# Six ring slots for gathers where there were eight, and two weight pairs kept for the second half of the prompt

## The chip, the cores and the metric

The kernel runs on one core of one Trainium2 chip. The metric is the device time of one execution in microseconds; the time of a kernel is the median of its runs.

## What is computed

One inference step of a small decoder with two layers, for a prompt of 512 tokens and eight samples of one token, all in float32 with a model width of 1024. Layer 0 mixes tokens with a gated short convolution and a dilated attention of eight heads, layer 1 with causal pooling. What takes most of the time stands in both layers after that: a retrieval of single-neuron experts. Each token makes eight queries, scores them against two sets of 128 subkeys, takes the 16 best of the 128 x 128 experts per head, and adds up 16 x 8 rows of a table, each weighed by the gelu of its dot product with the token:

```python
def peer_ffn(h, wq, subkeys, u_tab, v_tab):
    ...
    q = (hb @ wq).reshape(chunk, PEER_HEADS, 2, PEER_HALF)
    s = einsum('nhcd,hckd->nhck', q, sk)
    sv, si = top_k(s, 16)
    cs, ci = top_k(sv[:, :, 0, :, None] + sv[:, :, 1, None, :], 16)
    expert = i1 * 128 + i2
    act = gelu(einsum('nd,nhkd->nhk', hb, u_tab[expert]))
    return einsum('nhk,nhkd->nd', softmax(cs) * act, v_tab[expert])
```

## The kernel before, in words

The prompt's 512 tokens are four tiles of 128, one token to a partition; the first half of the prompt is tiles 0 and 1, the second half tiles 2 and 3. A *task* is one head of one tile, 16 *uses*; the samples' task at the end of each layer has eight. That makes 520 uses to a layer and 1040 in all. For each use GpSimd (POOL) gathers one expert for every token: 128 rows of 2048 floats, the expert's row of `u` and of `v` side by side, into one slot of `RING` (line 937). Slot `use % SLOTS` is used over and over, and the gather waits until the use `SLOTS` before it has been worked off (lines 932 to 935: `v_freed` from TensorE, `x_freed` for the few that VectorE adds itself). When the rows have landed, VectorE makes the dot products (line 2041), ScalarE the gelu, the gate and a diagonal matrix of the gates (lines 1502, 1507, 1511), and TensorE multiplies the diagonal with the rows of `v` into an accumulator (line 1310), which frees the slot.

All other work (the projections, attention and pooling of a half prompt, the queries and their scores) is cut into *pieces*. `agenda()` puts the pieces between the uses: while the experts of one half are being summed, the pieces of the next half are worked off. Every engine goes through the same list of pieces in order, SyncE (SP) too.

SP loads the weights. They come in pairs of 128 columns each, 1 MB a pair. `pair_homes()` gives each pair a buffer (its *home*): homes 0 and 1 are the two buffers of `WCH`, 2 and 3 lie in the ring's memory before the gathers begin, and 4 to 7 are places in `SC`, `H`, `VN` and `KT` that are free once, for four of layer 0's query pairs. For `WCH` a pair is loaded as soon as TensorE has closed the last piece that used the pair before it in that home (`AFTER`, in SP's `front`). A layer has eight query pairs (16 chunks, pieces `("q", l, b, hc)`); each half of the prompt (`b` = 0, 1) needs all eight. Before, every half loads all of them.

Until `ring_cleared` (set by VectorE once the samples' rows of the first mixer have been stored) the ring's memory holds other things. POOL's first gather waits for it, and for the first indices. POOL then issues in order, and SP, too, issues in order: a wait there holds all loads and small moves that stand behind it. Among those are the moves of the samples' scores from `YT` to `SC` (line 835).

Of the kernel before, what the change touches and what calls it, by code (L numbers as in the profile page):

```python
# [30 lines left out]
P = 128  # L31
D = 1024
KD = D // P
# [10 lines left out]
HC = 2 * PH  # L44
# [12 lines left out]
NW_FIRST = 4  # L57
NW_ONCE = 4
# [3 lines left out]
HT_N = BN + B  # L62
NB = 5
ACC_BANKS = (6, 4)
SLOTS = 8
ROW = 2 * D
DVE_LAG = 3
ADD_AT = 3
# [176 lines left out]
EARLY = 4  # L245
# [144 lines left out]
def pair_homes():  # L390

    chunks = chunk_list()
    cut = chunks.index(("q", 0, 0, 0)) // 2
    last, homes, after = {}, [], {}
    for n in range(len(chunks) // 2):
        once = n - cut - NW
        if 0 <= once < NW_ONCE:
            homes.append((NW_FIRST + once, 0))
            continue
        usable = range(NW_FIRST if n < cut else NW)  # L400
        home = min(usable, key=lambda b: last.get(b, b - NW_FIRST))
        if home in last:
            after[last[home]] = n
        last[home] = n
        homes.append((home, sum(h == home for h, _ in homes)))
    return homes, after
# [14 lines left out]
def build(nc, x_prompt, x_sample, state_conv, state_win_k, state_win_v, state_pool, norm_mix, w_in_ab,  # L421
# [5 lines left out]
    with ctx:  # L427
        def sb(name, shape, dt=f32):
            return ctx.enter_context(nc.sbuf_tensor(name, shape, dt))

        def sem(name):
            return ctx.enter_context(nc.semaphore(name))
# [3 lines left out]
        Hv = H[:, :].rearrange("p (s d) -> p s d", d=D)  # L436
        HT = sb("HT", [P, KD, HT_N])
        SC = sb("SC", [P, T * HC * NK + 2 * NK])
        RING = sb("RING", [P, SLOTS * ROW])
        WCH = sb("WCH", [P, NW, 2, KD, WC])  # L440
        KT = sb("KT", [P, CA, SEQ])
        VN = sb("VN", [P, T, DA])
# [54 lines left out]

        rows = RING[:, :].rearrange("p (s n) -> p s n", n=ROW)
        hrep = (H[:, BT * D + D:BT * D + 2 * D], KT[:, :, :].rearrange("p c n -> p (c n)")[:, 0:D])

        KV = 2 * DA
        kv = RING[:, 0:NKV * KV].rearrange("p (a t n) -> p a t n", a=NKV, t=2)
        o = NKV * KV
# [44 lines left out]
        o += B  # L548
        own_probs = RING[0:B * NH, o:o + NH]
        o += NH  # L550
        assert o <= SLOTS * ROW

        UW = BN + 2
        o = BT * HC * NK
# [35 lines left out]
        CHUNKS = chunk_list()  # L590
        HOMES, AFTER = pair_homes()
# [8 lines left out]
        g_loaded = sem("g_loaded")  # L600
        small_loaded = sem("small_loaded")
        sk_loaded = sem("sk_loaded")
        w_loaded = [sem(f"w_loaded{n}") for n in range(NW_FIRST + NW_ONCE)]
        kv_loaded = [sem(f"kv_loaded{n}") for n in range(NKV + 2)]
        pool_loaded = sem("pool_loaded")
        sample_moved = [sem(f"sample_moved{n}") for n in range(2)]
# [32 lines left out]
        sexp_ready = sem("sexp_ready")  # L639
        landed = [sem(f"landed{s}") for s in range(SLOTS)]  # L640
        ring_cleared = sem("ring_cleared")
# [46 lines left out]
        def pair_buffer(home):  # L688

            once = home - NW_FIRST  # L690
            if home < NW:
                return WCH[:, home, :, :, :]
            if home < NW_FIRST:
                return wch_first[:, home - NW, :, :, :]
            area = H[:, 3 * D:5 * D] if once == 2 else SC[:, (2 + once) * 2 * D:(3 + once) * 2 * D]
            return area.rearrange("p (t k n) -> p t k n", t=2, k=KD)

# [18 lines left out]
        def wait_chunk(eng, piece):  # L716
            n, which = divmod(CHUNKS.index(piece), 2)
            home, use = HOMES[n]
            eng.wait_ge(w_loaded[home], 16 * (use + 1) if home < NW_FIRST + 3 else 32)
            return [chunk_column(home, which, k) for k in range(KD)]  # L720

        block = ctx.enter_context(nc.Block())
# [2 lines left out]
        def _(sp):  # L725
# [5 lines left out]
            def load_pair(n):  # L731
                piece = CHUNKS[2 * n]
                if piece[0] == "p":
                    src = w_in_ab[0, ("bcxqkv".index(piece[2]) * CA + piece[3]) // 2]
                elif piece[0] == "v":
                    src = w_in_ab[0, (5 * CA + piece[2]) // 2]
                elif piece[0] == "wo":
                    src = w_out_ab[0, piece[2] // 2]
                else:
                    src = peer_wq[piece[1], piece[3] // 2]  # L740
                home = HOMES[n][0]
                if home == NW_FIRST + 3:
                    for which in range(2):
                        part = split_chunk(which)
                        sp.dma_start(part, src[:, which, :, :].rearrange("p (a b) n -> p a b n", a=part.shape[1])
                                     ).then_inc(w_loaded[home], 16)
                else:
                    sp.dma_start(pair_buffer(home), src).then_inc(w_loaded[home], 16)
# [26 lines left out]
            def front(piece):  # L775
                kind = piece[0]
                if piece == ONCE_AT:
                    wait_full(sp, piece)
                    for n in range(len(HOMES)):
                        if HOMES[n][0] >= NW_FIRST:  # L780
                            load_pair(n)
                if piece in CHUNKS and CHUNKS.index(piece) % 2 and CHUNKS.index(piece) // 2 in AFTER:
                    wait_full(sp, piece)
# [13 lines left out]
                if kind == "kn":  # L797
                    t = piece[1] * BT + piece[2]
# [17 lines left out]
                if kind == "so" and piece[1] in (4, 5):  # L816
                    t = BT + piece[1] - 4
# [59 lines left out]
        def _(pool):  # L877
# [51 lines left out]
            def gather(tau, k):  # L929

                use = first(tau) + k
                if use >= SLOTS and by_vector(use - SLOTS):
                    pool.wait_ge(x_freed, vector_rows(use - SLOTS) + 1)
                elif use >= SLOTS:
                    pool.wait_ge(v_freed, tensor_rows(use - SLOTS) + 1)
# [1259 lines left out]
```

## Time and profile before

| | us |
|---|---|
| median of 3 runs | 2979.59 |
| lowest and highest run | 2979.23, 2981.12 |
| the profiled execution | 2981.27 |
| its span (first to last instruction) | 2979.3 |
| PE busy | 2586.0 (87%) |
| VectorE busy | 2077.1 (70%) |
| GpSimd busy | 1223.5 (41%) |
| moved by DMA | 1213.29 MB, mean 407 GB/s |

The first gather is issued at 214.6 us, layer 0's uses end near 1640 us, and the rest is layer 1. Busy shares are means over the whole run; the part from 214 us on, in which the gathers run, is read by itself below. A PE that is busy 87% has its own waits inside that, since the ends of matmuls are modelled. "To landing" of a DMA is the time from its issue to its last byte's semaphore.

### The profile page before, as it was taken

What the parts mean: (1) busy time and instruction counts of PE and PEld (TensorE: products, weight loads), DVE (VectorE), ACT (ScalarE), POOL (GpSimd) and SP (SyncE); (2) the same over time, 40 slices, a digit from 0 to 9 for tenths busy, and PEclk for the clock granted to TensorE, in tenths of its full rate; (3) what the DMA queues carried; (4) which work ended last, traced back from release to release, by engine and by line L of the source; (5) the groups of instructions that cost most, each with busy time, mean ns of one, the idle gap of its engine ahead of it and who ended that gap; (6) DMA issues with size and microseconds to landing.
All of it is one profiled execution on the core that took longest, in us unless ns stands there. A gap on an engine that the chain in (4) does not pass through costs nothing.

```text
span 2979.3 us, 26395 instructions
## 1 busy us (share of the span) xinstructions
PE 2586.0 (87%) x7285; PEld 1274.0 (43%) x7285; DVE 2077.1 (70%) x4938; ACT 1281.6 (43%) x3753; POOL 1223.5 (41%) x1104
## 2 busy tenths in 40 slices
PE   8999998999988888888988888788999978778787
PEld 7675564555444443334444333333444422222222
DVE  3657766887766667776667677777666766677666
ACT  2123435655434435444444444445443444444444
POOL 2013543444444434444444444445434444444442
PEclk9999999999999999999999999999999999999999
DMA  9979999999999999999999999999999999999997
GB/s 356 366 278 381 405 421 412 422 400 406 421 421 421 421 420 396 421 421 421 421 421 421 411 410 414 421 418 414 416 421 420 419 416 412 421 419 417 421 414 331
DMA packets 174565, 1213.29 MB, mean 407 GB/s; under 512 B 19685, under 2 KB 20721, under 8 KB 32843
## 3 DMA queue, kind: packets, MB, share of 16 engines
q0 software_dynamic: 155904, 1124.11, 91.6%
q1 hardware_dynamic: 18515, 87.51, 7.6%
q8 instruction: 58, 0.95, 0.1%
q14 instruction: 88, 0.72, 0.1%
HBM read 1206.90 MB, written 38.37 MB: 418 GB/s over the span
## 4 chain that ended last, share of the span: by engine, by line
DMA 46%; PE 36%; DVE 8%; ACT 6%; issue 3%; POOL 1%; ACTq 0%; POOLq 0%; DVEq 0%
DMA RING<-in_peer_uv,idx 45%; PE PSUM L1310 22%; PE PSUM L989 9%; DVE RING L2041 4%; ACT diag L1511 2%; ACT L1502 1%; ACT gate L1507 1%; DMA RING<-in_peer_uv,pidx 1%; PE PSUM L1000 1%; POOL RING L937 1%; PE PSUM L971 1%; ACT act_h L1502 1%; ACT L1490 1%; PE PSUM L1298 1%; PE PSUM L1088 0%
## 5 line engine op out<-in xcount | busy, mean ns | idle before, releaser
L1310 PE MATMUL PSUM<-RING,diag 128*128 128x512 f32 (+1 forms) x4032 | 1955.0, 622 | 359.7 <-ACT diag L1511 353.7
L937 POOL DMA_INDIRECT RING<-in_peer_uv,idx x1024 | 1171.8, 1144 | 1544.3 <-PE PSUM L1310 1413.2
L2041 DVE CUSTOM_DVE_ANT_0 RING<-RING,H 128x1024 f32<-128x1024 f32 x1032 | 1262.7, 1224 | 700.8 <-DMA RING<-in_peer_uv,idx 694.7
L1310 PEld LDWEIGHTS PSUM<-RING,diag 128*128 128x128 f32 (+1 forms) x4032 | 732.9, 193 | 1420.9 <-ACT diag L1511 784.3
L1502 ACT ACTIVATE act_h<-dots 128x1 f32<-128x1 f32 x1040 | 208.1, 200 | 1110.4 <-DVE dots L2041 1108.9
L1511 ACT ACTIVATE diag<-ident,gate 128x128 f32<-128x128 f32 x992 | 398.3, 402 | 33.0 <-PE PSUM L1310 0.5
L989 PE MATMUL PSUM<-HT,WCH 128*128 128x256 f32 (+2 forms) x1408 | 335.0, 385 | 1.4 <-ACT HT L1363 1.3
L989 PEld LDWEIGHTS PSUM<-HT,WCH 128*128 128x128 f32 x1408 | 266.5, 193 | 94.5 <-issue 62.7
L1507 ACT ACTIVATE gate<-act_h,ex 128x1 f32<-128x1 f32 x992 | 292.2, 295 | 32.3
L1502 ACT ACT_TABLE_LOAD x90 | 115.5, 1283 | 5.6 <-DVE dots L2041 4.0
L1363 ACT ACTIVATE YT<-PSUM 128x256 f32<-128x256 f32 (+4 forms) x70 | 27.3, 391 | 173.2 <-PE PSUM L989 157.8
L2041 DVE DVE_READ_ACCUMULATOR2_ANT dots<- 128x1 f32 x1040 | 85.9, 83 | 0.0
L1490 ACT ACT_TABLE_LOAD x66 | 84.7, 1283 | 1.2
L1382 ACT ACTIVATE H<-H,negm 128x128 f32<-128x128 f32 (+3 forms) x32 | 18.0, 562 | 97.8 <-DVE negm L1743 97.6
L1298 PEld LDWEIGHTS PSUM<-SKT,YT 128*128 128x128 f32 (+1 forms) x316 | 41.4, 172 | 33.8 <-issue 29.6
L1298 PE MATMUL PSUM<-SKT,YT 128*128 128x128 f32 (+1 forms) x316 | 49.2, 279 | 0.0
L971 PE MATMUL PSUM<-ident,H 128*128 128x128 f32 (+1 forms) x200 | 33.6, 288 | 17.2 <-POOL POOL_STATE_M L886 9.7
L926 POOL DMA_DIRECT2D out_win_v_sample<-in_state_win_v x16 | 9.8, 617 | 91.5 <-PE PSUM L989 58.5
L989 PE MATMUL PSUM<-HT,RING 128*128 128x264 f32 x192 | 44.6, 389 | 0.0
L2019 DVE TENSOR_TENSOR onehot<-cij,iota 128x512 f32<-128x512 uint32 x65 | 44.6, 687 | 0.0
L2022 DVE TENSOR_TENSOR onehot<-onehot,si 128x512 f32<-128x512 f32 x65 | 44.6, 686 | 0.0
L2024 DVE TENSOR_REDUCE picked<-onehot 128x32 f32<-128x512 f32 x65 | 44.3, 681 | 0.0
(265 smaller groups left out, 1533.7 us busy)
## 6 DMA issues: line engine op xcount, KB each, us to landing
WCH<-in_peer_wq SPq DMA_DIRECT2D x28, 1024.0 KB, 9.1
WCH<-in_w_in_ab SPq DMA_DIRECT2D x18, 1024.0 KB, 9.8
RING<-in_peer_uv,idx POOLq DMA_INDIRECT x1024, 15.0
out_win_k_sample<-in_state_win_k POOLq DMA_DIRECT2D x8, 2016.0 KB, 12.7
out_win_v_sample<-in_state_win_v POOLq DMA_DIRECT2D x8, 2016.0 KB, 11.9
RING<-in_w_in_ab SPq DMA_DIRECT2D x6, 1024.0 KB, 11.5
WCH<-in_w_out_ab SPq DMA_DIRECT2D x6, 1024.0 KB, 9.8
X<-in_x_prompt SPq DMA_DIRECT2D x4, 512.0 KB, 4.3
```

The lines of the kernel that those rows point to most:

```text
L937: pool.indirect_dma_start(rows[:, use % SLOTS, :], None, peer_uv.rearrange("l e n -> (l e) n"), bass.IndirectOffsetOnAxis(ap=at, axis=0),) ...
L971: last = nc.tensor.transpose(out[0:cols, n * width:n * width + rows], src, ident[0:rows, 0:rows])
L989: last = nc.tensor.matmul(out[:, lo:width], w[k], rows[:, k, lo:width], start=(k == 0), stop=(k == KD - 1))
L1298: last = nc.tensor.matmul(out[0:m, j * P:(j + 1) * P], qp[:, hc % 2, j * P:j * P + m], SKT[:, hc, :], start=True, stop=True)
L1310: last = nc.tensor.matmul(PSUM[0:out_n, accumulator(n) + half, :], diag[:, at % DIAGS, 0:out_n], rows[:, use % SLOTS, D + half * 512:D + h ...
L1490: nc.scalar.activation(ex[:, par, :], cs[:, par, :], ACT.Exp, bias=ncs[:, par:par + 1], accum_out=exsum[:, par:par + 1]).then_inc(gates_ex ...
L1502: chain(nc.scalar.activation(act_h[:, st, column], dots[:, st, column], ACT.Gelu))
L1507: chain(nc.scalar.activation(gate[:, st, column], act_h[:, st, column], ACT.Copy, scale=weight))
L1511: nc.scalar.activation(diag[:, at % DIAGS, 0:n], selector, ACT.Copy, scale=gate[:, st, column]).then_inc(diag_ready, 1)
L2019: left(V.tensor_tensor(onehot[:], cij[:].unsqueeze(3).to_broadcast([P, 2, TOP, TOP]), iota16[:].unsqueeze(1).unsqueeze(1).to_broadcast([P, ...
L2022: left(V.tensor_tensor(onehot[:], onehot[:], si[:].unsqueeze(2).to_broadcast([P, 2, TOP, TOP]), ALU.mult))
L2041: V.tensor_tensor_reduce(out=u, in0=u, in1=row, scale=1.0, scalar=0.0, op0=ALU.mult, op1=ALU.add, accum_out=dots[:, tau % SETS, k:k + 1]). ...
```

## The change

`SLOTS` goes from 8 to 6, so a gather waits for the use six before it. The two slots that come free stay in `RING` behind the six, as homes 8 and 9. They hold the query pairs of heads 6 and 7, which are chunks 12 to 15. Layer 0's are loaded once SP comes to the piece `("sc", 0, 0, 3)`, after a wait for `ring_cleared`, and layer 1's once layer 0's second half has used the old ones. Both halves of the prompt multiply with them; the second half loads none for these chunks. Since six of the eight query pairs now go through the other homes, the second half's input pairs move up in `WCH`.

```diff
-SLOTS = 8
+SLOTS = 6
+KEPT = 2
...
     for n in range(len(chunks) // 2):
+        kind, *at = chunks[2 * n]
+        kept = at[2] // 2 - (HC // 2 - KEPT) if kind == "q" else -1
+        if kept >= 0:
+            home = NW_FIRST + NW_ONCE + kept
+            if at[1] == 0 and home in last:
+                after[last[home]] = n
+            last[home] = n
+            homes.append((home, at[0]))
+            continue
...
-        RING = sb("RING", [P, SLOTS * ROW])
+        RING = sb("RING", [P, (SLOTS + KEPT) * ROW])
...
+            if once >= NW_ONCE:
+                kept = SLOTS + once - NW_ONCE
+                return RING[:, kept * ROW:(kept + 1) * ROW].rearrange("p (t k n) -> p t k n", t=2, k=KD)
...
-            eng.wait_ge(w_loaded[home], 16 * (use + 1) if home < NW_FIRST + 3 else 32)
+            eng.wait_ge(w_loaded[home], 32 if home == NW_FIRST + 3 else 16 * (use + 1))
...
-                        if HOMES[n][0] >= NW_FIRST:
+                        if NW_FIRST <= HOMES[n][0] < NW_FIRST + NW_ONCE:
                             load_pair(n)
+                if piece == ("sc", 0, 0, EARLY - 1):
+                    sp.wait_ge(ring_cleared, 1)
+                    for n in range(len(HOMES)):
+                        if HOMES[n][0] >= NW_FIRST + NW_ONCE and CHUNKS[2 * n][1:3] == (0, 0):
+                            load_pair(n)
```

On SP, where the gathers begin, before (`in_peer_wq` are query pairs, `in_w_in_ab` input pairs of the second half, a row of 128x2048 is one pair of 1 MB):

```order
L748 DMA WCH<-in_peer_wq 128x2048
L835 DMA SC<-YT 8x256 x2
L748 DMA WCH<-in_peer_wq 128x2048
L835 DMA SC<-YT 8x256 x10
L748 DMA WCH<-in_w_in_ab 128x2048
L835 DMA SC<-YT 8x256 x2
L748 DMA WCH<-in_w_in_ab 128x2048
L835 DMA SC<-YT 8x256 x2
```

and now:

```order
L761 DMA WCH<-in_w_in_ab 128x2048
L853 DMA SC<-YT 8x256 x2
L761 DMA WCH<-in_w_in_ab 128x2048
L761 DMA RING<-in_peer_wq 128x2048 x2
L853 DMA SC<-YT 8x256 x14
```

The two input pairs stand where the two query pairs stood, and the two query pairs follow them into the ring's memory ahead of the small moves.

On SP, at the second half of layer 1, before:

```order
L748 DMA WCH<-in_peer_wq 128x2048
L835 DMA SC<-YT 8x256 x2
L748 DMA WCH<-in_peer_wq 128x2048
L835 DMA SC<-YT 8x256 x2
L748 DMA WCH<-in_peer_wq 128x2048
L835 DMA SC<-YT 8x256 x2
L748 DMA WCH<-in_peer_wq 128x2048
L835 DMA SC<-YT 8x256 x2
L748 DMA WCH<-in_peer_wq 128x2048
L835 DMA SC<-YT 8x256 x2
L748 DMA WCH<-in_peer_wq 128x2048
L835 DMA SC<-YT 8x256 x6
```

and now:

```order
L761 DMA WCH<-in_peer_wq 128x2048
L853 DMA SC<-YT 8x256 x2
L761 DMA WCH<-in_peer_wq 128x2048
L853 DMA SC<-YT 8x256 x2
L761 DMA WCH<-in_peer_wq 128x2048
L853 DMA SC<-YT 8x256 x2
L761 DMA WCH<-in_peer_wq 128x2048
L853 DMA SC<-YT 8x256 x10
```

Of the loads between the moves of this half, the last two are gone; layer 0's second half loses two in the same way.

On POOL, the first gathers, before (the names in brackets are the semaphores that the instruction waits for):

```order
L937 DMA RING<-in_peer_uv,idx 128x2048 [waits first_picked,ring_cleared]
L937 DMA RING<-in_peer_uv,idx 128x2048 x7
L937 DMA RING<-in_peer_uv,idx 128x2048 [waits v_freed,idx_ready]
L937 DMA RING<-in_peer_uv,idx 128x2048 [waits v_freed] x5
L937 DMA RING<-in_peer_uv,idx 128x2048 [waits x_freed]
```

and now:

```order
L955 DMA RING<-in_peer_uv,idx 128x2048 [waits first_picked,ring_cleared]
L955 DMA RING<-in_peer_uv,idx 128x2048 x5
L955 DMA RING<-in_peer_uv,idx 128x2048 [waits v_freed] x2
L955 DMA RING<-in_peer_uv,idx 128x2048 [waits v_freed,idx_ready]
L955 DMA RING<-in_peer_uv,idx 128x2048 [waits v_freed] x3
L955 DMA RING<-in_peer_uv,idx 128x2048 [waits x_freed]
```

Six gathers go out at once where eight did, and from the seventh on each waits for a slot.

## Rows read from the trace of the kernel before

**Rows 1.** The page's slices: DMA share in tenths, and GB/s, 40 slices.

```profile
DMA  9979999999999999999999999999999999999997
GB/s 356 366 278 381 405 421 412 422 400 406 421 421 421 421 420 396 421 421 421 421 421 421 411 410 414 421 418 414 416 421 420 419 416 412 421 419 417 421 414 331
```

**Rows 2.** The page's chain that ended last, by engine and by line.

```profile
DMA 46%; PE 36%; DVE 8%; ACT 6%; issue 3%; POOL 1%; ACTq 0%; POOLq 0%; DVEq 0%
DMA RING<-in_peer_uv,idx 45%; PE PSUM L1310 22%; PE PSUM L989 9%; DVE RING L2041 4%; ACT diag L1511 2%; ACT L1502 1%; ACT gate L1507 1%; DMA RING<-in_peer_uv,pidx 1%; PE PSUM L1000 1%; POOL RING L937 1%; PE PSUM L971 1%; ACT act_h L1502 1%; ACT L1490 1%; PE PSUM L1298 1%; PE PSUM L1088 0%
```

**Rows 3.** Stretches: length, each engine's busy us (xcount), PE clock, DMA share, GB/s.

```profile
214.00:640.00 426.00, 394.14 (x1302) 229.51 (x1301) 314.46 (x760) 203.35 (x555) 180.09 (x151) 0.97 0.99 404
640.00:1300.00 660.00, 577.15 (x1631) 289.09 (x1630) 484.83 (x1114) 299.04 (x868) 287.54 (x247) 0.97 1.01 417
1300.00:1640.00 340.00, 304.24 (x828) 146.31 (x826) 231.85 (x565) 145.28 (x448) 145.74 (x130) 0.98 1.01 421
1640.00:2960.00 1320.00, 1109.04 (x2625) 462.11 (x2624) 931.83 (x2195) 584.11 (x1754) 577.55 (x513) 0.97 1.01 417
```

**Rows 4.** Line 937, its gathers in the same four stretches, in order.

```profile
L937 POOL DMA_INDIRECT RING<-in_peer_uv,idx x151: 932/940/2768, 214.6 to 637.8; - x151
DMA to landing us min/median/max: 5.4/11.9/19.9
DMA to landing us min/median/max: 5.8/14.5/23.7
DMA to landing us min/median/max: 10.1/15.7/18.8
DMA to landing us min/median/max: 9.6/15.3/20.6
```

**Rows 5.** Timeline of DVE, 1149 to 1162 us: start, us, what, idle before.

```profile
1151.07 1.23 DVE L2041 CUSTOM_DVE_ANT_0 RING<-RING,H 128x1024 f32<-128x1024 f32 x1 [0.48 <-DMA RING<-in_peer_uv,idx]
1153.53 1.23 DVE L2041 CUSTOM_DVE_ANT_0 RING<-RING,H 128x1024 f32<-128x1024 f32 x1 [0.35 <-DMA RING<-in_peer_uv,idx]
1156.01 1.23 DVE L2041 CUSTOM_DVE_ANT_0 RING<-RING,H 128x1024 f32<-128x1024 f32 x1 [0.38 <-DMA RING<-in_peer_uv,idx]
1159.08 1.22 DVE L2041 CUSTOM_DVE_ANT_0 RING<-RING,H 128x1024 f32<-128x1024 f32 x1 [1.43 <-DMA RING<-in_peer_uv,idx]
```

**Rows 6.** Timeline of POOL, two gathers, at 600 and at 1151 us.

```profile
600.77 0.94 POOL L937 DMA_INDIRECT RING<-in_peer_uv,idx  x1 [10.05 <-PE PSUM L1310]
...
1151.38 1.73 POOL L937 DMA_INDIRECT RING<-in_peer_uv,idx  x1 [0.30 <-PE PSUM L1310]
```

**Rows 7.** Line 937 in 236-316, 480-545, 595-722, 1135-1170, 1290-1300, 1800-1812 us.

```profile
DMA to landing us min/median/max: 6.4/8.7/10.0
DMA to landing us min/median/max: 8.9/10.7/15.9
DMA to landing us min/median/max: 5.4/9.9/12.2
DMA to landing us min/median/max: 5.8/8.5/14.8
DMA to landing us min/median/max: 9.0/9.8/10.1
DMA to landing us min/median/max: 9.6/10.0/10.9
```

**Rows 8.** Stretch 320 to 352 us, columns as in rows 3.

```profile
320.00:352.00 32.00, 32.00 (x104) 17.39 (x104) 20.92 (x50) 13.94 (x43) 15.41 (x13) 1.00 1.00 415
```

**Rows 9.** Timeline of SP's queue, 214 to 222 us.

```profile
218.41 1.41 SPq L835 DMA_DIRECT2D SC<-YT  x2
220.27 0.34 SPq L748 DMA_DIRECT2D WCH<-in_peer_wq  x1
```

**Rows 10.** Timeline of DVE, the copy of the samples' scores at 258 us.

```profile
258.27 0.27 DVE L1882 COPY YT<-PSUM 8x128 f32<-8x128 f32 x1
```

More of the change, by code:

```diff
@@ L550, in build @@
         o += NH
-        assert o <= SLOTS * ROW
+        assert o <= (SLOTS + KEPT) * ROW
         UW = BN + 2
@@ L602, in build @@
         sk_loaded = sem("sk_loaded")
-        w_loaded = [sem(f"w_loaded{n}") for n in range(NW_FIRST + NW_ONCE)]
+        w_loaded = [sem(f"w_loaded{n}") for n in range(NW_FIRST + NW_ONCE + KEPT)]
         kv_loaded = [sem(f"kv_loaded{n}") for n in range(NKV + 2)]
```

## The prediction

> **What bounds the kernel now.** I read the page's slices first, then the chain that ended last, then the stretches. From the fourth slice on the 16 DMA engines are busy nine tenths or more, and in many slices they move 421 GB/s [rows 1]. The chain that ended last is 45% waiting for the gathers into the ring and 36% PE [rows 2]. So the gathers' bytes set the pace: a gather is 128 rows of 8 KB, 1.049 MB, and 1.049 MB / 421 GB/s = 2.49 us. VectorE's products show it: where they wait for nothing but the landing they start 2.46 and 2.48 us apart [rows 5].
>
> The second thing to see is how far ahead the ring lets the gathers run. One lap of a slot has two parts: from issue to landing, and the rest (product, gelu, gate, diagonal, matmul, and POOL's next issue). The stretches give the pace [rows 3], the landings their median [rows 4]:
> - 214 to 640 us: 151 gathers in 426 us, 2.82 us each, a lap of eight 22.6 us; landing takes 11.9, the rest 10.7.
> - 640 to 1300: 2.67 each, lap 21.4, landing 14.5, rest 6.9.
> - 1300 to 1640: 130 in 340, 2.62 each, lap 20.9, landing 15.7, rest 5.2.
> - 1640 to 2960: 513 in 1320, 2.57 each, lap 20.6, landing 15.3, rest 5.3.
>
> The shortest landing of the run is 5.4 us [rows 4]: a gather issued into an empty queue. What a landing takes above 5.4 us is other transfers standing ahead, and that is the reserve that keeps the DMA engines busy while POOL waits for a slot.
>
> **The change part by part.**
>
> *Fewer bytes.* The order of SP shows four loads of 1 MB gone: each layer's last two query pairs are fetched for the first half of the prompt and not again for the second. One costs 2.49 us of the DMA engines. Layer 0's places in SP's order are taken by the loads behind them, which move up in `WCH`, so the queue is empty of two loads where the second half's first pairs of layer 1 stood, about 1640 us, and of the last two of layer 1. There the DMA share is full [rows 1, 3] and nothing else is the limit: 4 x 2.49 = 10.0 us gained, hidden only where the DMA engines stop for another reason.
>
> *Two loads move forward.* The second half's first two input pairs are now loaded at the places where before's query pairs 12 to 15 were, and these go into the ring behind `ring_cleared`. So 2 MB leave the stretch from 320 to 352 us, where the DMA share is full but PE too is busy 32.00 of 32.00 us [rows 8], and go to about 220 to 240 us. There six gathers are issued at first where it was eight, so the bytes up to there are the same ten MB. The gain is 0 if PE is the limit at 320 to 352, 2 x 2.49 = 5.0 us if DMA is; both are full there, I take the middle, 2.5.
>
> *The new wait on SP.* SP waits for `ring_cleared` ahead of these two loads. POOL's first gather, behind the same semaphore, is issued at 214.6 us [rows 4], and SP's instruction just ahead of the wait is the load at 220.27 us [rows 9], so the wait has ended before SP comes to it: nothing. Behind it on SP's queue stand the moves of the sample's scores, issued from 218 us on [rows 9]. Behind 2 MB that share the engines with gathers, they land up to 4 x 2.49 = 10 us later; the VectorE copy that needs the next pair of them out of the way is at 258.27 us [rows 10]. That is cover of over 20 us, so nothing again; without it the opening would lose up to 10 us. The tail of the change, where layer 1's kept pairs are loaded after layer 0's second half has used them, moves loads within the same stretch: nothing.
>
> *Two slots fewer.* This is the term to weigh. At the same pace a lap of six leaves for the landing: 16.9 - 10.7 = 6.2 us from 214 to 640, 16.0 - 6.9 = 9.1 to 1300, 15.7 - 5.2 = 10.5 to 1640, 15.4 - 5.3 = 10.1 after. Against 5.4 needed, layer 1 keeps nearly 5 us to spare and the first stretch 0.8. So the loss sits in layer 0's first half and wherever POOL was held up for long, as at 600.77 us, where it had waited 10.05 us for PE [rows 6].
>
> To size it, go by the dips. A gather that lands L after its issue had L - 5.4 us of queue ahead of it. Two slots fewer take 2 x 2.49 = 4.98 us out of the queue, so the engines stand still for 10.4 - L wherever L is under 10.4. Each dip is charged once, at its shortest landing [rows 7]: 236 to 316 us: 10.4 - 6.4 = 4.0; 480 to 545: 1.5; 595 to 722: 5.0; 1135 to 1170: 4.6; about 1295: 1.4; about 1807: 0.8. Sum 17.3 us. Once lost, the time is given to every gather behind it, so a dip is not charged per gather.
>
> Upward: two dips are long. The first holds 28 gathers, 4.7 laps of six, with a median of 8.7 us: 1.7 per lap is 8.0, 4.0 more than charged. The third holds 45 gathers and may empty the queue twice, 5.0 more. That makes 26.3. A row also says that 5.4 is too kind: the gather issued at 1151.38 [rows 6] came 4.6 us ahead of the product at 1156.01, and yet its own product starts 3.07 us after that one and not 2.48 [rows 5], so the pace is lost 0.6 us earlier than 5.4 gives it; 0.6 for six dips is 3.6, together 30. Downward: the first stretch has PE busy 394 of 426 us [rows 3], and if PE hides the first two dips, 17.3 - 5.5 = 11.8. All of it vanishes only if the rest of a lap shrinks as landings come later, which it can where a landed row lay waiting for VectorE. I take the middle of 17.3 and 26.3, 21.8, since the long dips are long in the rows, and the PE that would hide them is what makes POOL wait.
>
> The shortest landing in the rows is 5.4 us [rows 4]. The Trainium skill, "DMA: Bandwidth & Descriptors", section "Anatomy of one DMA — SWDGE (gpsimd) path", gives a transfer issued by GpSimd 2.0 us plus its bytes at 436 GB/s; for a gather that is an estimate of 4.4 us, and no gather of this trace landed under 5.4. By 4.4 the threshold would be 9.4 and the dips 3.0 + 0.5 + 4.0 + 3.6 + 0.4 = 11.5 us, which with the two gains would make the change even. The measured 5.4 decides.
>
> *Sum:* 21.8 - 10.0 - 2.5 = +9.3 us. On the profiled execution of 2981.27 us (span 2979.3 and 2.0 around it) that is 2990.6; the median of the runs is 1.7 lower, 2979.59, so 2988.9, called 2989.
>
> **The rivals.**
> 1. *The ring was deeper than needed* (ends faster). The point is the rest of the lap from 214 to 640 us: 10.7 us, of which much may be rows that had landed and waited for VectorE and PE. If later landings take it from that waiting, six slots turn over in time, and the loss stays under 6.5 us; at 2.5 the sum is -10.0, 2969.6. For it: PE is near full there [rows 3]. Against it: landings of 5.4 and 5.8 us, an empty queue already with eight slots [rows 4, 7]. 0.13.
> 2. *A draw.* Only the dips outside PE's full stretches count, 11.8, and 11.8 - 12.5 = -0.7: 2979, and within 0.2% (6 us, about what a measurement can tell from no change) for losses from 6.5 to 18.5. 0.25.
> 3. *Every lap of the first stretch is short.* If each of the 151 / 6 = 25 laps lacks the 1.7 us of the first dip, that is 43, with the three later dips 4.6 + 1.4 + 0.8 = 50, and +37 in the sum: 3017. Against it: half the gathers there land in over 11.9 us [rows 4], above the threshold. 0.08.
> 4. That the four loads don't go: excluded by the order of SP.
>
> **How the numbers follow.** My forecast, a loss of 18.5 to 30 against 12.5 or less gained, +6 to +20 us or 2986 to 3000 with 2989 the likeliest, has 0.54. Slower is this with rival 3, 0.62; same 0.25; faster 0.13. The range leaves out rival 1 and most of rival 3: 2974 to 3003.
>
> **What would show it.** Right: four weight loads fewer; landings of the gathers near 10 us in layer 1 where they were 15.3, with the DMA share as full as before and that part some 10 us shorter; layer 0 longer by 10 to 20 us, with the DMA share lower from 214 to 720 and about 1140, and landings of 5.4 there more often. The forecast is wrong if layer 0 up to 1300 us keeps its length (rival 1), or if VectorE's waits for landings grow in layer 1 too.

## The result, and the profile after

The changed kernel takes 3027.14 us (median of five runs, 3022.52 to 3030.89); the kernel before, on the same chip, 2980.20 (2979.23 to 2981.15). The ratio is 1.0146, with an interval of 1.0136 to 1.0157: 46.9 us slower. The sign was forecast, the size (+9) was not. The profiled execution took 3022.52 us with a span of 3020.8, 41 more than before.

The page's slices of the kernel after, DMA share in tenths and GB/s, to be laid beside [rows 1], and the line of its packets:

```profile
DMA  9979999999999999999999999999999999999998
GB/s 352 365 284 385 377 415 393 369 364 353 416 412 409 416 422 393 419 395 418 422 421 417 396 402 401 421 417 415 417 414 419 418 413 421 419 414 420 418 413 356
DMA packets 173989, 1209.10 MB, mean 400 GB/s; under 512 B 19621, under 2 KB 20657, under 8 KB 32779
```

The bytes are 4.19 MB fewer, as the change says. But slices 7 to 10 (about 450 to 755 us) move 393, 369, 364 and 353 GB/s where they moved 412, 422, 400 and 406. The DMA share in tenths still reads 9 in all four: this digit hides a loss of a tenth, and GB/s shows it.

The stretches of the kernel after, columns as in [rows 3]:

```profile
214.00:420.00 206.00, 193.98 (x657) 116.40 (x656) 147.29 (x359) 84.12 (x251) 84.57 (x72) 0.98 0.99 385
420.00:500.00 80.00, 69.89 (x209) 39.25 (x208) 52.41 (x122) 35.71 (x98) 28.60 (x26) 0.94 1.01 414
500.00:580.00 80.00, 68.34 (x219) 37.62 (x218) 54.26 (x126) 43.63 (x105) 31.39 (x26) 0.96 0.94 361
580.00:680.00 100.00, 88.00 (x279) 48.26 (x277) 76.16 (x182) 51.35 (x127) 38.09 (x33) 0.95 0.93 371
680.00:760.00 80.00, 67.93 (x228) 38.57 (x229) 62.03 (x150) 41.10 (x100) 33.05 (x26) 0.94 0.92 353
...
1680.00:3000.00 1320.00, 1110.01 (x2633) 462.77 (x2633) 932.43 (x2199) 585.38 (x1759) 577.45 (x516) 0.98 1.01 414
```

And those of the kernel before that stand against the third to fifth:

```profile
500.00:580.00 80.00, 77.28 (x257) 43.12 (x258) 63.66 (x157) 52.13 (x127) 35.89 (x31) 1.00 1.00 413
580.00:680.00 100.00, 89.86 (x298) 50.03 (x296) 85.70 (x203) 56.53 (x137) 42.70 (x35) 0.95 0.99 406
680.00:760.00 80.00, 77.23 (x262) 45.26 (x260) 60.14 (x142) 39.36 (x107) 34.61 (x31) 0.98 0.99 408
```

The loss is local. Over these 260 us the kernel before moves 408.8 GB/s on average, the kernel after 362.4; to move the same bytes after takes 260 x 408.8 / 362.4 = 293 us, 33 more. No engine is fuller for it: PE, VectorE and ScalarE all do less. How much later than in the kernel before VectorE makes the product of a use, its shift, says the same (one execution of each kernel; the times in brackets are those of before). Use 96 (499 us) is 4.2 us late, use 192 (767 us) 36.0, use 416 (1360 us) 45.5, use 544 41.5, use 784 41.2 and the last 41.5. So 32 of 41 us are lost in uses 96 to 191, most of them with pieces of the second half's attention between them (these stand at uses 86 to 168), another 9.5 from there to 1360 us, and behind that 4.0 are given back, where layer 1's loads are gone.

The waits in that stretch, after (500 to 755 us; engine, line, what it waited for, us in total, times, longest):

```profile
POOL RING L955 <- PE PSUM L1328: 138.6, 66, 10.1
DVE RING L2059 <- DMA RING<-in_peer_uv,idx: 52.6, 42, 6.0
ACT act_h L1520 <- DVE dots L2059: 51.1, 30, 4.4
...
ACT H L1400 <- DVE negm L1761: 37.1, 13, 5.6
PEld PSUM L1328 <- ACT diag L1529: 22.5, 14, 4.1
```

The same uses in the kernel before (497 to 722 us):

```profile
POOL RING L937 <- PE PSUM L1310: 114.8, 62, 10.1
...
ACT act_h L1502 <- DVE dots L2041: 35.6, 20, 7.3
ACT H L1382 <- DVE negm L1743: 26.9, 13, 3.1
...
DVE RING L2041 <- DMA RING<-in_peer_uv,idx: 13.9, 21, 1.6
PEld PSUM L1310 <- ACT diag L1511: 13.0, 14, 2.8
```

VectorE's wait for landings goes from 13.9 to 52.6 us. But ScalarE waits longer for VectorE too, PE's weight loads for ScalarE, and POOL for PE. Every link of the way from a landing back to the next gather has grown, which is what a closed lap looks like: no engine is always busy, each waits for the next. But idle times grow in any stretch in which the same work takes longer, so the rows alone do not show a lap; the experiments have to.

The chain of waits of the kernel after shows one such lap (start, us, what; pieces between left out):

```profile
551.39 11.42 DMA RING<-in_peer_uv,idx
...
562.84 0.04 DVE RING L2059
...
564.68 0.48 DVE H L1757
...
565.18 0.56 DVE negm L1760
...
565.96 0.61 ACT H L1400
...
566.59 1.28 ACT L1520
...
568.45 0.41 ACT diag L1529
...
568.90 3.37 PE PSUM L1328 x4
572.27 1.73 PE PSUM L1007 x8
574.00 3.43 PE PSUM L1328 x8
...
581.41 1.45 POOL RING L955
...
583.17 8.55 DMA RING<-in_peer_uv,idx
```

A gather lands at 562.8 and VectorE makes its product (line 2059). Only behind that, in VectorE's order, stand the mask and the maximum of one attention step (lines 1757 to 1761), since VectorE's products run three uses ahead of the pieces (`DVE_LAG`). ScalarE's exponential (line 1400) waits for the maximum, and behind the exponential stand the gates and diagonals of rows that landed long before; behind the diagonals stand PE's matmuls, which free the slots. So a late landing holds back slots that have nothing to do with it.

What that does to the next gathers, POOL's timeline of the kernel after (start, us, what, idle before):

```profile
563.76 1.11 POOL L955 DMA_INDIRECT RING<-in_peer_uv,idx  x1 [0.78 <-PE PSUM L1328]
573.06 0.94 POOL L955 DMA_INDIRECT RING<-in_peer_uv,idx  x1 [8.18 <-PE PSUM L1328]
575.99 0.97 POOL L955 DMA_INDIRECT RING<-in_peer_uv,idx  x1 [1.99 <-PE PSUM L1328]
577.71 0.94 POOL L955 DMA_INDIRECT RING<-in_peer_uv,idx  x1 [0.75 <-PE PSUM L1328]
581.41 1.45 POOL L955 DMA_INDIRECT RING<-in_peer_uv,idx  x1 [2.77 <-PE PSUM L1328]
583.17 1.03 POOL L955 DMA_INDIRECT RING<-in_peer_uv,idx  x1 [0.30 <-issue]
```

and the last two products of those, on VectorE:

```profile
585.43 1.23 DVE L2059 CUSTOM_DVE_ANT_0 RING<-RING,H 128x1024 f32<-128x1024 f32 x1 [1.38 <-DMA RING<-in_peer_uv,idx]
...
589.22 1.23 DVE L2059 CUSTOM_DVE_ANT_0 RING<-RING,H 128x1024 f32<-128x1024 f32 x1 [1.62 <-DMA RING<-in_peer_uv,idx]
```

Worked out from the landing records, the four gathers issued at 573.06, 575.99, 577.71 and 581.41 land at 578.55, 581.88, 585.41 and 589.19: after 5.5, 5.9, 7.7 and 7.8 us, and each 3.3 to 3.8 us behind its predecessor instead of 2.49. This is where the forecast's threshold breaks. A landing of 7.7 us has over 2 us of queue ahead of it by my 5.4, and yet the pace was lost four times running.

The waits of layer 1 show nothing of the sort: VectorE waits for landings as in the kernel before. First after (1680 to 3000 us), then before (1640 to 2960 us):

```profile
DVE RING L2059 <- DMA RING<-in_peer_uv,idx: 370.3, 457, 3.8
```

```profile
DVE RING L2041 <- DMA RING<-in_peer_uv,idx: 371.2, 456, 3.5
```

### The profile page after: what moved, and what is told of

It reads as the page before. It is cut to its first block, busy times and chain, and to the rows that moved or that the text cites. A ratio compares the mean times of both kernels' runs of the same rounds, so it can differ in the third digit from the quotient of the medians.

```text
span 3020.8 us, 26391 instructions
## 1 busy us (share of the span) xinstructions
PE 2598.1 (86%) x7285; PEld 1274.3 (42%) x7285; DVE 2079.9 (69%) x4938; ACT 1285.5 (43%) x3753; POOL 1214.5 (40%) x1104
## 4 chain that ended last, share of the span: by engine, by line
DMA 40%; PE 38%; ACT 9%; DVE 8%; issue 3%; POOL 1%; SPq 0%; DVEq 0%; ACTq 0%; POOLq 0%
DMA RING<-in_peer_uv,idx 39%; PE PSUM L1328 24%; PE PSUM L1007 9%; DVE RING L2059 5%; ACT diag L1529 2%; ACT L1520 2%; ACT gate L1525 2%; ACT L1508 1%; ACT act_h L1520 1%; PE PSUM L989 1%; POOL RING L955 1%; PE PSUM L1316 1%; DMA RING<-in_peer_uv,pidx 1%; PE PSUM L1018 1%; PE PSUM L1106 0%
## 5 line engine op out<-in xcount | busy, mean ns | idle before, releaser
L1007 PE MATMUL PSUM<-HT,WCH 128*128 128x256 f32 (+2 forms) x1152 | 270.7, 382 | 1.6 <-ACT HT L1381 1.4
L1007 PEld LDWEIGHTS PSUM<-HT,WCH 128*128 128x128 f32 x1152 | 216.8, 192 | 75.7 <-issue 49.7
L1007 PE MATMUL PSUM<-HT,RING 128*128 128x264 f32 (+1 forms) x448 | 108.0, 390 | 0.0
L1007 PEld LDWEIGHTS PSUM<-HT,RING 128*128 128x128 f32 x448 | 84.1, 192 | 24.1 <-issue 12.5
L989 PEld LDWEIGHTS PSUM<-ident,H 128*128 128x128 f32 (+1 forms) x200 | 24.7, 156 | 54.1 <-DVE den L1768 20.6
## 6 DMA issues: line engine op xcount, KB each, us to landing
out_win_v_sample<-in_state_win_v POOLq DMA_DIRECT2D x8, 2016.0 KB, 11.2
```

Source lines behind the costliest of these rows:

```text
L989: last = nc.tensor.transpose(out[0:cols, n * width:n * width + rows], src, ident[0:rows, 0:rows])
L1007: last = nc.tensor.matmul(out[:, lo:width], w[k], rows[:, k, lo:width], start=(k == 0), stop=(k == KD - 1))
```

## The experiments

In all of them the ratio is to the kernel before on the same chip. The theories: **depth** (two slots fewer make the whole loss, the loads a gain of some 10), against something else in the change; then, once depth was seen, what in uses 96 to 191 makes it cost so much, the **engines' own load** or the **closed lap** of waits just read.

**Depth alone.** In the kernel before, with its eight slots and all its loads, a gather waits also for the use six (e1) or seven (e2) before it, and in e3 the use six before it in uses 96 to 191 alone:

```diff
-                if use >= SLOTS and by_vector(use - SLOTS):
-                    pool.wait_ge(x_freed, vector_rows(use - SLOTS) + 1)
-                elif use >= SLOTS:
-                    pool.wait_ge(v_freed, tensor_rows(use - SLOTS) + 1)
+                lag = 6
+                freed = dict.fromkeys(by_vector(use - n) for n in (SLOTS, lag) if use >= n)
+                for vector in freed:
+                    at = max(use - n for n in (SLOTS, lag) if use >= n and by_vector(use - n) == vector)
+                    if vector:
+                        pool.wait_ge(x_freed, vector_rows(at) + 1)
+                    else:
+                        pool.wait_ge(v_freed, tensor_rows(at) + 1)
```

(e2: `lag = 7`; e3: `lag = 6 if 96 <= use < 192 else SLOTS`.)

> The kernel before with its eight slots and all its weight loads, but each gather also waits for the use six before it, so that at most six are under way. If the ring's depth alone makes the loss, this shows the measured +47 us without the 10 us of saved loads: 3035 to 3042 us, with most of it between uses 96 and 192. If the kept pairs and the moved loads make it (a weight load that now stands in the way at the start, or of the second half's input pairs), this stays within 10 us of before, 2980 to 2990. By the sum of dips on record it would be 2980 + 22 = 3002.

> As the run with six, but each gather waits for the use seven before it. By the dips of the prediction one slot fewer moves the threshold to 7.9 us: 1.5 + 2.5 + 2.1 = 6 us, 2986. If every lap of the stretch of attention pieces pays, the seventh slot is worth a fifth to a half of what two are: 2990 to 3005.

> The wait for the use six before only in uses 96 to 191, in which the changed kernel's products fell back by some 30 us; eight elsewhere. If the loss is made there, +25 to +32: 3005 to 3012. If it is a slower rate of the DMA engines with fewer gathers under way, it is spread over the run and these 9% of the uses cost about 5 us: 2985.

Measured, against 2983.89 for the kernel before: e1 3043.58 (1.0195, 1.0178 to 1.0212), e2 2996.70 (1.0043, 1.0026 to 1.0060), e3 3017.39 (1.0112, 1.0093 to 1.0131). Depth alone costs 59.7 us at six and 12.8 at seven, so the second slot costs more than three times what the first does. The dips on record gave 22 and 6. Most of the price at six is paid in uses 96 to 191: the shift of e1's products goes from 10.1 to 45.7 us there, and e3, which has six only there, loses 33.5. The rest of the change (the moved loads, the new wait on SP, the kept pairs' places) is not needed to explain the sign, nor the place where most is lost.

**The loads alone.** e4 has eight slots and does not load the last two query pairs of each layer for the second half; the identity stands in for them:

```diff
+        if kind == "q" and at[1] == 1 and at[2] >= HC - 4:
+            homes.append((-1, 0))
+            continue
...
+            if home < 0:
+                return [ident[:, :]] * KD
```

> The kernel before with eight slots, but the second half's last two query pairs of each layer are not loaded: the four chunks are multiplied with the identity matrix, so those heads choose other experts. Four loads of 1 MB fewer and nothing else. If the DMA engines are the limit where they stood, 4 x 2.49 = 10 us less: 2970. If they are hidden, 2980.

Measured 2974.51 (0.9965, 0.9951 to 0.9979), 9.4 us faster; the sum said 10.0. e1's loss less this gain is 50.3, the change itself lost 46.9: the two parts account for it to within 3.4 us, less than the intervals of e1 and e4 leave open.

**One slot, one pair.** e9 is the change with `SLOTS = 7` and `KEPT = 1`.

> The changed kernel with seven slots and one kept pair per layer: two loads fewer in place of four. The wait for the use seven before cost 12.8 us by itself, two loads give back 5.0, the one moved load 0 to 2.5: 2985 to 2989 where before is 2980; by the sum on record (a dip rule with 7.9 us for a threshold, 6 us lost) about even, 2979.

Measured 2986.95 against 2982.15 (1.0016, 1.0006 to 1.0025): 4.8 us slower. Half the exchange loses as well, if little: e2's 12.8 less two loads, 5.0, would be 7.8.

**The engines' load.** e5 leaves out half of the matmul's columns in uses 96 to 191 on PE (but for a task's first and last use), e7 half of the dot product's columns on VectorE. These two have eight slots and serve as yardsticks; e6 and e8 are the same with the wait of e3.

```diff
-                for half in range(2):
+                for half in range(1 if 96 <= use < 192 and 0 < k < steps(tau) - 1 else 2):
```

```diff
+                if 96 <= use < 192:
+                    u, row = u[:, 0:D // 2], row[:, 0:D // 2]
```

> The kernel before, eight slots, but in uses 96 to 191 TensorE leaves out the second half of the sum's columns (512 of 1024), except in a task's first and last use. This is the yardstick for the next run: TensorE has some 80 us less to do there. The stretch is 2.8 us per use against 2.49 for its bytes, so at most 25 us can go: 2960 to 2975.

> The same columns left out, and the wait for the use six before in uses 96 to 191. If slots are lost because TensorE holds them while it works on the second half's attention, the 33 us that this wait cost in full shrink to under 15 beside the yardstick. If fewer gathers under way slow the DMA engines themselves, whoever holds the slots, the cost stays near 33.

> The kernel before, eight slots, but in uses 96 to 191 VectorE's dot product takes 512 of 1024 columns, some 0.55 us less per use, 51 us in all. Yardstick for the next run: 2960 to 2980.

> The same shorter dot product, and the wait for the use six before in uses 96 to 191. If VectorE is what holds the slots there, the 33 us shrink to under 15 beside its yardstick; if TensorE is, they shrink only by what a lap is shorter, to 20 to 30; if it is the DMA engines' own rate, they stay near 33.

Measured: e5 2981.50 (0.9994, 0.9983 to 1.0006), e6 3004.80 (1.0072, 1.0050 to 1.0095), e7 2980.93 (0.9994, 0.9983 to 1.0005), e8 3003.41 (1.0066, 1.0043 to 1.0089). The yardsticks did not fall, so with eight slots neither engine sets the time there, and my expectations missed, for e5 by 6 us and for e7 by 1. Six slots cost 23.3 us beside e5 and 22.5 beside e7, where they cost 33.5 in full: each relief takes a third. That is neither the 15 or less of an engine that holds the slots nor the 33 of a rate that the DMA engines set by themselves; only e8's bound of 20 to 30, for slots held by TensorE, was met, and e6 does not bear it out. e15 and e16 have both reliefs at once.

> The kernel before, in which uses 96 to 191 leave out half of the dot product's columns on VectorE and half of the columns of the matmul on PE (e5 and e7 together). It is the yardstick of e16: 2970 to 2982 us by either theory.

> e15 with the wait for the use six before in uses 96 to 191 alone. Theory of the engines' load (the two engines together fill the laps): each relief alone took ten of the 33.5 us, so both take twenty or more, and at most 14 us remain beside e15. Theory of the closed lap: the waits between the engines stay, and 16 us or more remain.

Measured: e15 2978.98 (0.9985, 0.9975 to 0.9995), e16 3000.21 (1.0047, 1.0030 to 1.0064). Still 21.2 us, with e16's four runs from 2996.02 to 3006.74. The work of both engines on the uses halved is worth no more than that of one, so this load is not what fills the lap, and that theory fell by its own bound of 14. One limit: PE was relieved by less than the columns left out, 32 us of busy time in e15, since its granted clock fell too. From 500 to 755 us the kernel before, e15 and e16 read:

```profile
500.00:755.00 255.00, 239.37 (x797) 135.53 (x798) 205.40 (x490) 146.63 (x364) 110.63 (x93) 0.97 1.00 408
```

```profile
500.00:755.00 255.00, 207.46 (x680) 123.52 (x679) 161.89 (x497) 148.11 (x367) 96.65 (x96) 0.89 1.00 414
```

```profile
500.00:755.00 255.00, 198.30 (x628) 115.39 (x626) 151.25 (x458) 140.91 (x341) 88.09 (x88) 0.86 0.95 381
```

**VectorE's lead.** If the exponential waits because the attention step stands behind a product three uses ahead, a lead of one should free it: e11 is the changed kernel and e12 the kernel before, with

```diff
-DVE_LAG = 3
+DVE_LAG = 1
```

> The changed kernel (six slots, two kept pairs), but VectorE works off each piece one use after its place in the list and not three (DVE_LAG 1 for 3). The theory: with six slots the products close a loop. VectorE takes a piece only after the product three uses on, whose gather is issued only when the use three before the piece's place is freed (3 - 6), so ScalarE and TensorE wait, through the piece, for a landing. With a lag of 1 that distance is 1 - 6 = -5, as with eight slots and a lag of 3. By it most of the 32 us lost between uses 96 and 192 come back: 2990 to 3008 where the changed kernel was 3027. If the loss is only the lap's length (landing and rest, whatever stands between), the lag changes little: 3020 to 3030.

> The yardstick: the kernel before with eight slots and a lag of 1. Its queue of gathers is never short for long, so little can come back; VectorE may now wait for TensorE's pieces where it did not: 2975 to 2990.

Measured against 2981.53: e11 3061.36 (1.0257, 1.0238 to 1.0277), e12 3026.59 (1.0147, 1.0125 to 1.0168). Both missed, and the test settles nothing, since a shorter lead makes new waits. e12's waits from 500 to 755 us:

```profile
ACT act_h L1502 <- DVE dots L2041: 110.0, 39, 8.4
PEld PSUM L1310 <- ACT diag L1511: 59.8, 36, 5.4
...
DVE H L1739 <- PE PSUM L1010: 34.3, 13, 7.7
```

VectorE now waits for PE's attention scores (line 1010) and the products behind it come late, with eight slots as with six.

**The lap cut.** e13 takes the second half's attention past VectorE. ScalarE takes the exponential straight from PE's bank and sums the row; mask, maximum and count weights of that half are left out. Neither the exponential on ScalarE nor PE's transposes behind it wait any longer for a step of VectorE's that stands behind a landing; gates and diagonals still wait for their own products. e14 is e13 with the wait of e3.

```diff
...
             def exponentials(b, m):
                 w = (b * BT + m // NH + 1) * P
+                if b:
+                    if m >= 2:
+                        wait_full(act, ("pT", b, m - 2))
+                    wait_full(act, ("s", b, m))
+                    emptied(nc.scalar.activation(S[:, m % 2, 0:w], bank(("s", b, m))[:, 0:w], ACT.Exp, scale=1.0 / 64,
+                                                 accum_out=den[:, (b * BT + m // NH) % 2, m % NH:m % NH + 1]),
+                            ("s", b, m))
+                    return
...
             def masked_scores(b, m):
+                if b:
+                    return
...
             def counted(b, m):
+                if b:
+                    return
...
```

> The kernel before (eight slots), in which the second half's attention no longer passes through VectorE: ScalarE takes the exponential straight from the scores' PSUM bank as soon as PE has filled it, and sums the row itself; the mask, the maximum and the count weights of the second half are left out. So neither ScalarE's exponential nor PE's transposes wait any longer for a step of VectorE's that stands behind a product, which in turn waits for its landing. It is the yardstick of e14. With eight slots the stretch is mostly set by DMA: 2965 to 2980 us by either theory.

> e13 with the wait for the use six before in uses 96 to 191 alone. Theory of the closed lap (a landing releases a product, behind it VectorE's attention step, behind that ScalarE's exponential and PE's transposes, and behind these the diagonals and matmuls of rows that landed long ago, which hold the slots): the lap is cut, so six slots cost at most 12 us beside e13, where e3 cost 33.5. Theory of the engines' load alone (VectorE has some 28 us less to do, as in e8): some 20 us or more remain, as in e6 and e8.

Measured: e13 2980.73 (0.9993, 0.9983 to 1.0002), e14 2997.05 (1.0037, 1.0023 to 1.0051). Six slots cost 16.3 us here: half of the 33.5 is gone, more than the relief of either engine took, but it lies between my two bounds of 12 and 20. e14's five runs go from 2990.33 to 2999.02, so beside e16's 21.2 alone the gap is not clear. The cut also takes work off VectorE: its busy time from 500 to 755 us is 183.63 us in e13 (row below) and 205.40 in the kernel before, 22 less. But the halved dot products of e15, the same as those of e7 and e8, take off 44 (161.89), and e8 kept 22.5. Both kinds of relief at once are e17 and e18:

> e13 and e15 in one: eight slots, the second half's attention past VectorE (its mask, maximum and count weights left out), and in uses 96 to 191 half the columns of the dot product and of the matmul left out. It is the yardstick of e18: 2970 to 2982 us by either theory.

> e17 with the wait for the use six before in uses 96 to 191 alone. Cutting the detour through VectorE left 16.3 us of 33.5 (e14 less e13), halving both engines' work left 21.2 (e16 less e15). If the two are separate parts of one lap (waits of one engine for another, and the engines' own work), at most 8 us remain beside e17. If what is left in e14 is something else than VectorE's and PE's work on the uses, such as the attention's and the projections' own pieces standing between the matmuls in PE's order, 13 us or more remain.

Measured against 2983.90: e17 2980.52 (0.9986, 0.9976 to 0.9996), e18 2989.52 (1.0014, 1.0005 to 1.0024). 9.0 us are left, a quarter, between my two bounds of 8 and 13. With both reliefs in place the cut lap thus takes 21.2 to 9.0, and here the runs are apart: e16's lowest is 2996.02, e18's highest 2993.29. The stretch from 500 to 755 us in e3, e13, e14, e17 and e18, in this order (columns as above):

```profile
500.00:755.00 255.00, 218.45 (x696) 121.27 (x696) 186.38 (x440) 134.19 (x324) 96.87 (x82) 0.93 0.93 358
```

```profile
500.00:755.00 255.00, 238.91 (x794) 134.61 (x793) 183.63 (x425) 146.55 (x374) 107.64 (x93) 0.98 1.00 415
```

```profile
500.00:755.00 255.00, 232.17 (x759) 128.12 (x758) 175.02 (x398) 143.29 (x359) 97.11 (x88) 0.97 0.96 388
```

```profile
500.00:755.00 255.00, 205.47 (x678) 117.99 (x678) 135.37 (x424) 147.15 (x373) 92.69 (x95) 0.92 1.01 418
```

```profile
500.00:755.00 255.00, 201.57 (x644) 113.50 (x644) 128.63 (x395) 143.89 (x361) 88.05 (x90) 0.89 0.98 397
```

With six slots the stretch moves 358 GB/s; with the lap cut 388 beside 415; with both 397 beside 418. The landing records say why in one number: of the 96 gathers of uses 96 to 191, so many were issued less than 5 us ahead of their predecessor's landing: 6 in the kernel before, 35 after, 27 in e3, 19 in e14, 13 in e18. Behind their predecessors these land later than the 2.49 us of full pace by 6.7 us in sum before and by 36.7 after: 30.0 of the 31.7 us that the 96 landings are slower by.

So the detour through VectorE's attention step, with the work that it holds, is shown as about half of the local loss (17.2 of 33.5, 12.2 of 21.2), and the engines' work on the uses as a further part: 12.3 us of the 33.5 with the detour, 7.3 of the 16.3 without it. The two may well act in one way, through the time from a landing to the next issue into its slot, the rest of a lap. Worked out from the landing records, its mean in uses 96 to 185 is 9.6 us in e3, 8.0 in e14, 8.0 in e16 and 6.7 in e18, where six slots cost 33.5, 16.3, 21.2 and 9.0. That the detour costs more than by making the lap longer is not shown. What the last 9 us are stays open. In both e17 and e18 the attention's and the projections' own pieces still stand between the matmuls in PE's order, and that was not tried apart.

**A version that keeps the slots.** e10 has eight slots and keeps nothing. Layer 1's second half takes its query chunks in another order, 12 to 15 first, and so uses the two pairs that the first half left in `WCH`: two loads fewer.

```diff
+def turned(l, b, n):
+    return (n - 4) % HC if (l, b) == (1, 1) else n
...
+        if chunks[2 * n] in (("q", 1, 1, HC - 4), ("q", 1, 1, HC - 2)):
+            home, use = homes[chunks.index(("q", 1, 0, chunks[2 * n][3])) // 2]
+            last[home] = n
+            homes.append((home, use))
+            continue
```

> The kernel before with eight slots and no kept pairs; but layer 1's second half takes its query chunks in the order 12 to 15, 0 to 11, so that it begins with the two pairs that its first half left in the two weight buffers (between them layer 1 loads no other pair). Two loads of 1 MB fewer, with no slot given up. If a load is worth 2.49 us wherever the DMA engines are the limit, 5.0 us less: 2975. If the two were hidden, or the later scores of head 0 hold up the search, 2980 or more.

Measured 2976.53 against 2982.15 (0.9981, 0.9972 to 0.9990), 5.6 us faster, where two loads of 2.49 us make 5.0. It is faster than both kernels of this case.

## Why the prediction was wrong, and where it was right

- **What bounds the kernel** was read rightly: bytes set the pace where the queue is full. Four loads gone were forecast at 10.0 us, and e4 gives 9.4.
- **The sign** came from the right term: depth costs more than the loads bring (e1, e2, e4, e9).
- **The opening** came out near, but in part by luck. The first dip (236 to 316 us) was charged 4.0 us, less 2.5 for the moved loads; at 480 us the shift is 3.8. e1, which moves no loads, is 7.1 us late there. By these two executions the dip cost more than 4.0 and the moved loads brought some 3 back. The two were not tried apart; no shift asks for a cost of SP's new wait.
- **The last two dips of layer 0** came about as charged. Read at the first product behind each time of the kernel before, the shift grows from 1135 to 1170 us by 4.6 (charged 4.6), from 1290 to 1300 by 2.5 (charged 1.4).
- **The step that failed** is "Each dip is charged once, at its shortest landing", in the second and third dips. Read in the same way, from 480 to 545 us it charged 1.5 and the shift grows by 12.8; from 595 to 722 it charged 5.0, with 5.0 more as an upper bound, and the shift grows by 14.4. With 1.6 us between them and 3.4 behind them, which were charged nothing, that is the 32 of uses 96 to 191. So the term "two slots fewer" stood at 21.8 us where e1 measured 59.7. Two things were wrong in it. First the threshold. I took 5.4 us, the shortest landing, for the point at which the engines run dry, and then saw in the row of 1151 us [rows 5, 6] that a gather issued 4.6 us ahead of its predecessor's product lost 0.6 us. I put 0.6 per dip into the bound, where that row says that the point lies near 5 us ahead of the predecessor, a landing of some 7.5 us and not 5.4: 2.1 for each of six dips, some 13 in place of 3.6. Nor was 5.4 an empty queue: the gather of that landing (603.41 us) was issued 2.8 us ahead of its predecessor's. Second, and larger, "charged once". A dip was taken for one gap, after which the queue is short but regular. Where attention steps stand between the uses the gaps go on, lap after lap. The chain above shows one way: the late landing delays the attention step behind it, that delays the exponential, the diagonals and the slots, and the next gathers are late again. In this stretch 13 exponentials wait for the maximum (the row of `negm` above), and with eight slots the reserve nearly covered them.
- **"The rest of a lap"** was taken as 10.7 us up to 640 us and 6.9 from there to 1300 [rows 3, 4]. The second stretch mixed two kinds of uses: in the kernel before the mean rest of uses 96 to 185 is 11.2 us, and 11.4 still in the last 40 of them, behind 640 us; in uses 192 to 299 it is 6.2. A use takes 2.79 us in uses 96 to 191, a lap of six 16.7, so 5.5 us were left for a landing all through this stretch, where the forecast saw 9.1 from 640 us on. With six slots the rest does shrink, as rival 1 hoped, but only to 9.4.
- **Rival 3** (every lap short, 3017) was nearest in mechanism, each lap paying again, and in size. It was put evenly on all laps from 214 to 640 us, with the rest of a lap as the measure. Up to use 96 (499 us) only 4.2 us were lost, though; the loss began where the attention pieces stand between the uses, and 15 of its 32 us came behind 640 us. Rival 1 fell with e1.
- **Layer 1**: landings were forecast near 10 us where they were 15.3 [rows 4]; worked out from the landing records their median is 10.2, and VectorE's waits for them did not grow (370.3 to 371.2 us). Its gain came as forecast at the places of the loads, 3.3 us at uses 512 to 544 and 3.8 at 768 to 784, but between these it gave 3.5 back, so that it is not 10 us shorter as I had written. e1, without the gain, loses 9 us there.

## What to carry to other kernels

In this kernel the reserve of the ring was not measured by its mean lap or by its shortest landing, but by the longest stretch in which slots are freed late, and by what a late landing holds up: follow the lap from a landing through every queue that works in order back to the next issue, and ask whether a queue puts work of another kind (here an attention step) behind the newest landing and ahead of the oldest slot. Where one did, two dips charged 6.5 us cost 27; at 1135 us, with no attention step about, the charge of 4.6 held. And bytes saved by giving up reserve are better saved by order: e10 reuses what is still in its buffer and gives up nothing.

## What the hardware showed that was not expected

**Pace falls before the queue is empty.** I took the gathers of the kernel after with no packet of 4 KB or more from another queue between their predecessor's landing and their own. Those issued 6 to 7 us ahead of the predecessor's landing follow it after 2.50 us on average (138 gathers), 5 to 6 us ahead after 2.53 (75), 4 to 5 after 2.92 (42), 3 to 4 after 3.17 (17), 2 to 3 after 3.36 (6). e1 gives 2.51, 2.57, 2.93, 3.30 and 3.48. So in this kernel a gather of 1 MB, which moves in 2.49 us, wants to be issued some 5 us ahead of the end of the one before it.

**A wait of PE can be paid twice.** In the lap above, PE had idled 3.69 us for a diagonal, and its next four matmuls took 3.37 us; four like them at 549.40 us took 1.73 by the chain. The timeline of PE in the kernel after, and the stretch with its clock:

```profile
563.33 1.89 PE L1007 MATMUL PSUM<-HT,WCH 128*128 128x256 f32 x8
568.90 3.37 PE L1328 MATMUL PSUM<-RING,diag 128*128 128x512 f32 x4 [3.69 <-ACT diag L1529]
```

```profile
568.00:572.00 4.00, 3.10 (x4) 1.42 (x5) 3.01 (x7) 3.87 (x9) 0.00 (x0) 0.57 1.00 424
```

The granted clock is at the lower of its two levels, 1.2 GHz, from 568.3 to 571.7 us, and at 2.4 before and after. From 500 to 760 us the kernel after has six such spells, 27 us in all, the kernel before two, 14 us. In or just ahead of each of the six PE had idled 1.7 to 4.9 us; not every such wait has one (1.72 us idle at 557 us has none). The mean matmul of line 1328 takes 633 ns there against 615, which over 288 of them is 5 us of the loss, inside the lap. In e17 and e18, which leave PE less to do, the clock's mean falls to 0.92 and 0.89, so relieving PE gives back part of what it takes: its matmuls are fewer and slower.
